# Reciprocal roots on 128x4, spread by turns, and a rotation taken at the eviction, in a two-layer hybrid mixer

## The chip, the cores and the metric

The kernel runs on one core of a Trainium2 chip. The metric is device time in microseconds (us), smaller is better. Three runs of the kernel before gave 2074.2, 2075.43 and 2074.64 us; their median is 2074.64 us. All times in this document are of this one core. PE is TensorE, DVE is VectorE, ACT is ScalarE, POOL is GpSimd.

## What is computed

Two layers of a hybrid mixer on 512 positions of width 1024, then a final norm. The parts that the change touches are the two norms of a layer, the retention branch with its rotation and its per-head normalization, and the retention gate:

```python
def rms_norm(x, g):
    y = x32 * lax.rsqrt(jnp.mean(x32 * x32, axis=-1, keepdims=True) + EPS)
    return (y * g)

def rotary(x, pos, rot_dim, theta):      # halves x1, x2 of each head
    return concat([x1 * cos - x2 * sin, x2 * cos + x1 * sin, rest])

def retention_mixer(z, gn_g):            # 4 heads of 128
    zq, zk, zv, zg = split(z, 4)
    q, k = rotary(zq, ...), rotary(zk, ...) * (dk ** -0.5)
    ...                                  # chunked causal retention -> o
    mu, var = mean(o), mean(square(o - mu))      # per position and head
    o = ((o - mu) * lax.rsqrt(var + EPS)) * gn_g
    return o * jax.nn.silu(zg)

def hybrid_layer(x, ...):
    h = rms_norm(x, norm1_g)
    z = h @ w_in                         # all branches' projections
    y_a, y_b, y_c, y_d = conv, attention, retention, pool branches
    merged = sum over branches of (branch @ w_branch) * sigmoid(z_gate + b_gate)
    x = x + merged @ w_o
    h = rms_norm(x, norm2_g)
    u_gate, u_val = split(h @ w_up, 2)
    return x + (silu(causal_dwconv(u_gate)) * u_val) @ w_down
```

## The kernel before

Features lie on the 128 partitions, the 512 positions on the free axis, so a "tile" is 128 features by 512 positions and fills one PSUM bank. Each projection tile is 8 chunks of three matmuls (`product`, L1189 to L1191): high weights by high data, high weights by low data, low weights by high data. PE walks a fixed list of weight groups: 12 of stage A (`A_TILES`: compressed keys and values, keys, values, four query tiles q0 to q3, the attention gate, an empty "pad"), 32 of stage B (`B_TILES`: the retention tiles rq, rk, rv, rg of each head, the convolution's c, h, b and the pool's u), then the branch merge, the output projection, the up projection (U) and the down projection. ACT makes the high half of each weight group (`ahead`, L456), POOL the low half (L434), DVE evicts each accumulator bank (`take`, L721) multiplied by `rstd`, the norm's reciprocal root, which stands as a full 128x512 tile with one value per column, the same on all partitions.

Norm: PE multiplies a matrix of ones by the 128x512 sums of squares (`sum_squares`, L1257), which gives the column sum on all 128 partitions; ACT takes the square root of 128x512 (`root`, L462), DVE the reciprocal of 128x512 (`inverse_root`, L752). That is done twice per layer (`sumsq1` after tile 2 of stage A, `sumsq2` after the first up tile). The retention heads do the same with L1435 (PE), L590 (ACT) and L968, L971 (DVE, in two halves), four times per layer.

Stage B runs attention (scores, softmax, values) and retention between the quarters of its projection tiles. A table `SIDE` has a slot for each quarter of each of the 32 tiles (slot 4b to 4b+3 for tile b); every engine walks the slots in order and does its own part of each step found there. So the table fixes the order on PE, DVE and ACT, and semaphores count the uses of shared things: two score banks `s` (list `S_USES`, a use may begin when the use two before it is freed), two turn banks `t`, two accumulators `acc` (`acc_free`).

The retention rotation (L757 to L765, `rotate`) takes the evicted rq or rk, has its two halves of 64 partitions exchanged into `rot` by two DMAs that ACT issues (L487, L488), multiplies `rot` by sine, the tile by cosine, and adds: three DVE operations in slots of the tile after next. The attention's own rotations of k0, k1 and q0 to q3 in stage A have the same three operations.

At the end of stage A, DVE evicts tile 10 (the attention gate), rotates q3, finishes the compressed keys (`kc`, L855), makes `center` (L856), reads the pad (L858), and then does step `gate` (L864), which frees the score bank that PE needs for its step `cmp_keys` (L1343).

Of the kernel before, what the change touches and what calls it, by code (L numbers as in the profile page):

```python
# [23 lines left out]
F32 = mybir.dt.float32  # L24
# [5 lines left out]
P = 128  # L30
S = 512
# [76 lines left out]
for _h in range(RH):  # L108
    _n0 = RET_SLOT[_h]
    for _m in range(QT):  # L110
        SIDE[_n0 + _m].append(("ret_scores", _h, _m))
        SIDE[_n0 + _m + 1].append(("ret_values", _h, _m))
    SIDE[_n0 + 5].append(("ret_gate", _h))
    SIDE[_n0 + 6].append(("ret_var", _h))
    SIDE[_n0 + 7].append(("ret_inverse", _h))
    SIDE[POOL_SLOT[_h]].append(("pool", _h))
for _h in range(RH):
    SIDE[RET_SLOT[_h] + (11, 8, 8, 10)[_h]].append(("ret_end", _h))
    SIDE[RET_SLOT[_h] + (12, 9, 9, 12)[_h]].append(("ret_hi", _h))
    SIDE[RET_SLOT[_h] + (14, 10, 10, 14)[_h]].append(("ret_split", _h))  # L120
# [4 lines left out]
for _b in range(B_GROUPS - 1):  # L125
    for _k in range(4):
# [4 lines left out]
        if B_TILES[_b][0] in ("rq", "rk") and _k < 2:  # L131
            SIDE[4 * (_b + 2) + (1 if B_TILES[_b][0] == "rq" else 0) + _k].insert(0, ("rotate", B_TILES[_b], _k))
# [6 lines left out]
S_USES = ["sumsq1", "hid_k", "hid_v", "kc", "vc", "kc_swap"]  # L139
S_USES += [_e for _e in SEQUENCE if _e[0] in ("gate", "cmp_keys", "cmp_scores", "scores", "ret_scores", "ret_var", "pool")]  # L140
S_USES += ["sumsq2"]
# [8 lines left out]
for _slot in SIDE:  # L150
    for _e in _slot:
        if _e[0] in ("cmp_scores", "scores", "ret_gate", "ret_var", "ret_hi", "attn_hi") or _e[0] == "conv" and _e[2] == 2 or _e[0] == "ret_values" and _e[2] == QT - 1:
            A_MADE.append(_e)
# [29 lines left out]
def build(nc, xT, weights, vec, w1, pool_w, consts, decay, out):  # L183
    with ExitStack() as ctx:
# [41 lines left out]
        rg_t = at("rg_t", [P, S], F32, W + 14 * KB)  # L226
# [20 lines left out]
        ssq = at("ssq", [P, S], F32, R + 10 * KB)  # L247
        R2 = R + 12 * KB
# [17 lines left out]
        half_b = small[:, 112:144]  # L266
        pad_out = small[:, 144:146]
# [43 lines left out]
        root_ready = sem("root_ready")  # L311
        ssq_zero = sem("ssq_zero")
# [38 lines left out]
        ROT_DMA = 16 * (3 * 4 + RH * 2)  # L351

        def rot_value(L, name):
            i = ROT[name] // 2
            return L * ROT_DMA + 16 * (4 * (i + 1) if i < 3 else 12 + 2 * (i - 2))
# [89 lines left out]
        def _(act):  # L445
# [12 lines left out]
            def root(use, L):  # L458
# [3 lines left out]
                nc.scalar.activation(rstd[:, :], s_of(use)[:, :], ACT.Sqrt, bias=C("eps", 1),  # L462
                                     scale=1.0 / D).then_inc(root_ready, 1)

            def rotate_partners(L, name):
# [16 lines left out]
                else:  # L482
                    act.wait_ge(acc_free, 1 + L * TILES + (A_GROUPS + B_TILES.index(name) + 2))
                    before = [n for n, k in ROT.items() if k == i - 2][0]
                    act.wait_ge(v_made, v_count(L, before))
                    src = (rq if name[0] == "rq" else rk)[:, name[1] % 2, :]
                    act.dma_start(dst[0:64, :], src[64:128, :]).then_inc(rot_ready[i % 2], 16)  # L487
                    act.dma_start(dst[64:128, :], src[0:64, :]).then_inc(rot_ready[i % 2], 16)  # L488
# [21 lines left out]
            with act.Fori(0, LAYERS) as L:  # L510

                for g in range(A_GROUPS):
# [4 lines left out]
                    if 1 <= g <= 4:  # L517
                        act.wait_ge(acc_free, 1 + L * TILES + g)
                        nc.scalar.activation((k_cmp[:, :], v_cmp[:, :], kT[:, 0, :], kT[:, 1, :])[g - 1], acc[(g - 1) % 2][:, :],
                                             ACT.Copy).then_inc(acc_free, 1)  # L520
                    for name in ("k0", "k1", "q0", "q1", "q2", "q3"):
# [10 lines left out]
                for b in range(B_GROUPS):  # L532
                    ahead(L, A_GROUPS + b)
                    if 0 < b and B_TILES[b - 1][0] in ("rq", "rk"):
                        rotate_partners(L, B_TILES[b - 1])
# [12 lines left out]
                    for n in range(4 * b, 4 * b + 4):  # L548
                        for e in SIDE[n]:
# [28 lines left out]
                            elif e[0] == "ret_gate":  # L578
# [32 lines left out]
                def up(i, g, loop=None):  # L611
                    for k in range(2):
# [7 lines left out]
                        if i is None and k == 0:  # L620
                            root("sumsq2", L)
# [1034 lines left out]
```

## Time and profile before

| | us |
|---|---|
| median of three runs | 2074.64 |
| the profiled execution, own time | 2072.95 |
| its span, first to last instruction | 2071.1 |
| PE busy in the span | 2043.2 (99%) |
| DVE busy | 1209.7 (58%) |
| ACT busy | 685.6 (33%) |
| POOL busy | 917.5 (44%) |

The profiled execution's own time is 1.69 us below the median of the runs. "Busy" of PE counts from the start of a matmul to its modelled end; matmuls overlap, so what one costs is read from the distance between the starts of its neighbours. A row of the timeline gives start and duration in us, engine, line, operation, the names written and read, shapes, a count, and in brackets how long the engine was idle before it and what it waited for.

### The profile page before, as it was taken

To read this page: it belongs to the slowest core of one execution; us is meant where nothing else is said; L and a number is where in the kernel's file an instruction comes from. 1 tells how busy PE (TensorE), PEld (TensorE's weight loads), DVE (VectorE), ACT (ScalarE), POOL (GpSimd) and SP (SyncE) were. 2 spreads that over 40 slices of the span, in tenths; PEclk is the share of its full clock that TensorE was granted. 3 is DMA by queue.
4 is the path that set the end of the run, shared out by engine and by line. 5 is a ranking of instruction groups with operands and counts; after the bars stand their busy time and mean duration, and the time that the engine had idled before them with its cause. 6 is when DMAs were issued, how large, how long until landed. Compare 5 with 4: busy or idle time off the path is not lost.

```text
span 2071.1 us, 31913 instructions
## 1 busy us (share of the span) xinstructions
PE 2043.2 (99%) x9800; PEld 1637.2 (79%) x9800; DVE 1209.7 (58%) x1799; ACT 685.6 (33%) x1007; POOL 917.5 (44%) x672
## 2 busy tenths in 40 slices
PE   9999999999999999999999999999999999999997
PEld 7777677888888888888887777778888888888886
DVE  7766865422327888862267677572322378888522
ACT  4355533323232322222233554333323232222222
POOL 3422233444445555545544212335444455555552
PEclk9999999999999999999999999999999999999998
DMA  5311132222232223223233112322223223232233
GB/s 210 99 60 52 55 91 91 96 92 101 91 101 92 96 97 101 92 94 111 93 126 96 53 51 64 95 89 95 101 91 101 91 93 101 92 101 96 100 105 108
DMA packets 57432, 194.90 MB, mean 94 GB/s; under 512 B 7040, under 2 KB 7552, under 8 KB 57216
## 3 DMA queue, kind: packets, MB, share of 16 engines
q1 hardware_dynamic: 52576, 186.17, 26.8%
q10 hardware_dynamic: 4768, 7.61, 1.5%
q8 instruction: 49, 0.80, 0.2%
q14 instruction: 39, 0.32, 0.1%
HBM read 186.67 MB, written 2.10 MB: 91 GB/s over the span
## 4 chain that ended last, share of the span: by engine, by line
PE 93%; DVE 4%; issue 1%; ACT 1%; DMA 0%; ACTq 0%; SPq 0%; DVEq 0%
PE acc L1189 28%; PE acc L1191 28%; PE acc L1190 28%; PE o L1389 2%; PE s L1363 2%; PE t L1371 1%; PE o L1428 1%; PE s L1418 1%; PE t L1409 0%; DVE win_k L779 0%; DMA w_raw<-weights_dram 0%; PE s L1444 0%; PE s L1435 0%; DVE rstd L752 0%; DVE sc L721 0%
## 5 line engine op out<-in xcount | busy, mean ns | idle before, releaser
L434 POOL TENSOR_TENSOR w_lo<-w_raw,w_hi 128x512 fp32r<-128x512 f32 x668 | 917.3, 1394 | 1129.6 <-ACT w_hi L456 1114.0
L1189 PE MATMUL acc<-xg_hi,w_hi 128*128 128x512 f32 x1904 | 769.5, 404 | 6.5 <-DVE sc L721 3.6
L1191 PE MATMUL acc<-xg_hi,w_lo 128*128 128x512 f32 x1904 | 742.9, 390 | 0.0
L1190 PE MATMUL acc<-xg_lo,w_hi 128*128 128x512 f32 x1904 | 741.8, 390 | 0.0
L456 ACT ACTIVATE w_hi<-w_raw 128x1024 fp32r<-128x1024 f32 x336 | 355.1, 1057 | 777.5 <-PE acc L1191 740.3
L1189 PEld LDWEIGHTS acc<-xg_hi,w_hi 128*128 128x128 f32 x1904 | 357.4, 188 | 116.5 <-issue 33.4
L1190 PEld LDWEIGHTS acc<-xg_lo,w_hi 128*128 128x128 f32 x1904 | 357.8, 188 | 77.1 <-issue 6.7
L1191 PEld LDWEIGHTS acc<-xg_hi,w_lo 128*128 128x128 f32 x1904 | 357.3, 188 | 76.4
L1066 DVE TENSOR_TENSOR work<-acc,rstd 128x512 f32<-128x512 f32 x64 | 44.1, 690 | 256.1 <-PE acc L1191 256.1
L1189 PE MATMUL acc<-act_hi,w_hi 128*128 128x512 f32 x352 | 136.9, 389 | 0.0
L1190 PE MATMUL acc<-act_lo,w_hi 128*128 128x512 f32 x352 | 136.9, 389 | 0.0
L1191 PE MATMUL acc<-act_hi,w_lo 128*128 128x512 f32 x352 | 136.9, 389 | 0.0
L1072 DVE SCALAR_TENSOR_TENSOR work<-work,acc 128x512 f32<-128x512 f32 x64 | 44.0, 687 | 103.1 <-PE acc L1191 103.1
L1160 DVE SCALAR_TENSOR_TENSOR x<-acc,x 128x512 f32 x16 | 11.1, 693 | 158.6 <-PE acc L1191 158.6
L1189 PE MATMUL acc<-y_hi,w_hi 128*128 128x512 f32 x256 | 99.6, 389 | 0.0
L1190 PE MATMUL acc<-y_lo,w_hi 128*128 128x512 f32 x256 | 99.6, 389 | 0.0
L1191 PE MATMUL acc<-y_hi,w_lo 128*128 128x512 f32 x256 | 99.6, 389 | 0.0
L624 ACT ACTIVATE work<-work 128x512 f32<-128x512 f32 x44 | 27.8, 632 | 190.3 <-DVE work L1115 190.3
L924 DVE COPY pT<-t 128x128 f32<-128x128 f32 (+3 forms) x128 | 56.8, 484 | 53.2 <-PE o L1389 53.1
L1191 PEld LDWEIGHTS acc<-act_hi,w_lo 128*128 128x128 f32 x352 | 66.1, 188 | 13.8
L1189 PEld LDWEIGHTS acc<-act_hi,w_hi 128*128 128x128 f32 x352 | 66.1, 188 | 13.7
L1190 PEld LDWEIGHTS acc<-act_lo,w_hi 128*128 128x128 f32 x352 | 66.1, 188 | 13.7
(208 smaller groups left out, 2238.1 us busy)
## 6 DMA issues: line engine op xcount, KB each, us to landing
w_raw<-weights_dram SPq DMA_DIRECT2D x339, 512.0 KB, 3.3
x<-xT_dram SPq DMA_DIRECT2D x8, 256.0 KB, 5.9
rot<-rq ACTq DMA_DIRECT2D x16, 128.0 KB
rot<-rk ACTq DMA_DIRECT2D x16, 128.0 KB
dec<-decay_dram ACTq DMA_DIRECT2D x8, 256.0 KB, 3.3
out_dram<-x SPq DMA_DIRECT2D x8, 256.0 KB, 2.7
con<-consts_dram SPq DMA_DIRECT2D x1, 1406.0 KB, 10.5
w1k<-w_dram SPq DMA_DIRECT2D x2, 512.0 KB, 8.7
```

Of the source, the lines that this page charges most:

```text
L434: nc.gpsimd.tensor_tensor(w_lo[:, slot, part], w_raw[:, slot, part], w_hi[:, slot, part].bitcast(F32), ALU.subtract).then_inc(lo_ready, 1)
L456: nc.scalar.activation(w_hi[:, slot, :], w_raw[:, slot, :], ACT.Copy).then_inc(hi_ready, 1)
L624: nc.scalar.activation(work[:, 2, :], work[:, 1, :], ACT.Tanh, scale=0.5).then_inc(silu_ready, 1)
L924: t_end(ve.tensor_copy(pT[:, u % 2, 0:w], t_of(e)[:, 0:w]), e)
L1066: ve.tensor_tensor(work[:, n, :], acc[n % 2][:, :], rstd[:, :], ALU.mult).then_inc(acc_free, 1)
L1072: ve.scalar_tensor_tensor(out=work[:, n, :], in0=work[:, n, :], scalar=1.0, in1=acc[n % 2][:, :], op0=ALU.add, op1=ALU.mult).then_inc(acc_ ...
L1189: mm(tile, w_h, right_hi, start=first, stop=False)
L1190: mm(tile, w_h, right_lo, start=False, stop=False)
L1191: return mm(tile, w_l, right_hi, start=False, stop=last)
L1363: mm(b[:, 0:w], qT[r, h % 4, qi * P:(qi + 1) * P], kT[r, br, 0:w], start=True, stop=True).then_inc(s_done, 1)
L1371: ins = nc.tensor.transpose(b[:, k * P:(k + 1) * P], pr_of(u)[:, k * P:(k + 1) * P], ident)
L1389: ins = mm(o_bank[qi % 2][d, j * P:(j + 1) * P], v[:, d], p[:, half, :], start=(br == 0 and k == 0), stop=(br == 1 and k == qi + 1))
```

## The change

Four things change.

1. The column sums are computed as four products of one column each: each 128-position block of the squares is the loaded operand, one column of ones the streamed one. Positions then lie on partitions and the sums are 128x4. ACT's root and DVE's reciprocal work on 128x4. Then PE turns each of the four columns, repeated 128 times, by a transpose (`spread_root`, `ret_spread`), which gives the 128x512 tile back. For the norms ACT copies it into `rstd`; for retention DVE reads it from the score bank in `ret_end`.
2. Once per layer, between `kc` and `center`, DVE makes `cos_rms` and `sin_rms`, `rstd` times cosine and sine. rq and rk are evicted times `cos_rms`; ACT copies the two halves from the accumulator bank crosswise into `rot` (two copies of 64x512, in place of two DMAs) and frees the bank; DVE multiplies `rot` by `sin_rms` and adds, both in the last slot of the next tile.
3. ACT's tangent of the retention gate (`ret_tanh`) moves from slot 5 to slot 2 of a head, DVE's use of it (`ret_gate`) from 5 to 4.
4. `ret_end`, `ret_hi` and `ret_split` get other slots.

The diff, cut to its core:

```diff
+    SIDE[_n0 + 2].append(("ret_tanh", _h))
+    SIDE[_n0 + 4].append(("ret_gate", _h))
     SIDE[_n0 + 6].append(("ret_var", _h))
     SIDE[_n0 + 7].append(("ret_inverse", _h))
+    SIDE[_n0 + 8].append(("ret_spread", _h))
...
-    SIDE[RET_SLOT[_h] + (11, 8, 8, 10)[_h]].append(("ret_end", _h))
+    SIDE[RET_SLOT[_h] + (9, 9, 9, 9)[_h]].append(("ret_end", _h))
...
-            SIDE[4 * (_b + 2) + (1 if B_TILES[_b][0] == "rq" else 0) + _k].insert(0, ("rotate", B_TILES[_b], _k))
+    if B_TILES[_b][0] in ("rq", "rk"):
+        SIDE[4 * (_b + 1) + 3].insert(0, ("rotate", B_TILES[_b]))
...
-                nc.scalar.activation(rstd[:, :], s_of(use)[:, :], ACT.Sqrt, bias=C("eps", 1),
+                nc.scalar.activation(root4, s_of(use)[:, 0:QT], ACT.Sqrt, bias=C("eps", 1),
                                      scale=1.0 / D).then_inc(root_ready, 1)
+            def root_spread(use, L):
+                act.wait_ge(s_done, s_use(L, use))
+                nc.scalar.activation(rstd[:, :], s_of(use)[:, :], ACT.Copy).then_inc(rstd_ready, 1)
...
+            def swap_halves(L, tile):
+                T, i = A_GROUPS + B_TILES.index(tile), ROT[tile]
+                act.wait_ge(v_made, v_count(L, ("took", *tile)))
+                nc.scalar.activation(rot[0:64, i % 2, :], acc[T % 2][64:128, :], ACT.Copy)
+                nc.scalar.activation(rot[64:128, i % 2, :], acc[T % 2][0:64, :], ACT.Copy).then_inc(acc_free, 1)
...
+                def inverse_root(n):
+                    dve.wait_ge(root_ready, 2 * L + (n + 1))
+                    s_end(ve.reciprocal(root4, root4), use, wait=True)
+                    alone(dve)
+                    dve.sem_inc(inverse_ready, 1)
+                    dve.wait_ge(rstd_ready, 2 * L + (n + 1))
...
                 def rotate_ret(e):
-                    rotate(e[1], (rq if kind == "rq" else rk)[:, h % 2, :], "cos_r", "sin_r", (e[2],))
+                    dve.wait_ge(acc_free, 1 + L * TILES + (T + 2))
+                    then(ve.tensor_tensor(r, r, sin_rms[:, :], ALU.mult))
+                    v_end(ve.tensor_tensor(z, z, r, ALU.add), e[1])
...
                 v_end(ve.tensor_tensor(kc[:, 0:NCMP], kc[:, 0:NCMP], kc_rot[:, 0:NCMP], ALU.add), "kc")
+                ve.tensor_tensor(cos_rms[:, :], rstd[:, :], C("cos_r", S), ALU.mult).then_inc(chain, 1)
+                then(ve.tensor_tensor(sin_rms[:, :], rstd[:, :], C("sin_r", S), ALU.mult))
                 v_end(ve.scalar_tensor_tensor(out=center[:, :], ...
...
-                    then(ve.reciprocal(pT[:, 1, 0:S // 2], pT[:, 1, 0:S // 2]))
-                    s_end(ve.reciprocal(pT[:, 1, S // 2:S], pT[:, 1, S // 2:S]), ("ret_var", e[1]), wait=True)
+                    s_end(ve.reciprocal(ret_inv, ret_inv), ("ret_var", e[1]))
...
+                    if kind in ("rq", "rk"):
+                        v_end(ve.tensor_tensor((rq if kind == "rq" else rk)[:, i % 2, :], acc[T % 2][:, :], cos_rms[:, :], ALU.mult),
+                              ("took", kind, i), wait=True)
...
-                    mm(b[:, :], ones, ssq[:, :], start=True, stop=True).then_inc(s_done, 1)
+                    for t in range(QT):
+                        ins = mm(b[:, t:t + 1], ssq[:, t * P:(t + 1) * P], ones[:, 0:1], start=True, stop=True)
+
+                def spread_root(use, value):
+                    pe.wait_ge(inverse_ready, value)
+                    b = s_begin(use)
+                    for t in range(QT):
+                        ins = nc.tensor.transpose(b[:, t * P:(t + 1) * P], spread(root4[:, t:t + 1], [[0, P]]), ident)
...
-                                   norm=("sumsq1", L * 16 + DC, 3) if g == 2 else None)
+                                   norm=("sumsq1", L * 16 + DC, 3, sum_squares) if g == 2 else
+                                   ("spread1", L * 2 + 1, 1, spread_root) if g == 3 else None)
...
+                def ret_spread(e):
+                    pe.wait_ge(s_free, 1 + s_use(L, ("ret_var", e[1])) + 1)
+                    b = s_begin(e)
+                    for t in range(QT):
+                        ins = nc.tensor.transpose(b[:, t * P:(t + 1) * P], spread(ret_inv[:, t:t + 1], [[0, P]]), ident)
```

`spread2` is placed in the second up tile in the same way, after its second quarter.

Two places show the order. On PE in tile 3 of stage A, between its second and third quarter, the program before has nothing but the tile's own matmuls:

```order
L1189 MATMUL acc<-xg_hi,w_hi 128x512
L1190 MATMUL acc<-xg_lo,w_hi 128x512
L1191 MATMUL acc<-xg_hi,w_lo 128x512
L1209 REGISTER_ALU
L1189 MATMUL acc<-xg_hi,w_hi 128x512
```

In the changed program the wait for the reciprocal, the wait for a score bank and the four turns stand there:

```order
L1223 MATMUL acc<-xg_hi,w_hi 128x512
L1224 MATMUL acc<-xg_lo,w_hi 128x512
L1225 MATMUL acc<-xg_hi,w_lo 128x512
L1296 ISA
L1274 REGISTER_ALU
L1300 MATMUL s<-con,small 128x128 x4
L1243 REGISTER_ALU
L1223 MATMUL acc<-xg_hi,w_hi 128x512
```

The four turns (L1300) are new on PE's queue, and the 12 matmuls of the tile's second half stand behind them. On DVE at the end of stage A, from the last step of q3's rotation to the attention gate's step, the program before has:

```order
L765 TENSOR_TENSOR qT<-qT,rot 128x512
L855 TENSOR_TENSOR kc<-kc,kc_rot 128x31
L856 SCALAR_TENSOR_TENSOR center<-con 128x128
L857 REGISTER_ALU
L858 COPY small<-acc 128x2
L726 REGISTER_ALU
L864 TENSOR_SCALAR gates<-s 128x96
```

and the changed one:

```order
L789 TENSOR_TENSOR qT<-qT,rot 128x512
L883 TENSOR_TENSOR kc<-kc,kc_rot 128x31
L884 TENSOR_TENSOR cos_rms<-rstd,con 128x512
L886 TENSOR_TENSOR sin_rms<-rstd,con 128x512
L681 REGISTER_ALU
L887 SCALAR_TENSOR_TENSOR center<-con 128x128
L888 REGISTER_ALU
L889 COPY small<-acc 128x2
L745 REGISTER_ALU
L895 TENSOR_SCALAR gates<-s 128x96
```

Two operations of 128x512 stand between `kc` and the step that frees the score bank (`gates`, L864 before, L895 now).

## Rows read from the trace of the kernel before

**Rows 1.** The page's first part: busy us and share of each engine.

```profile
PE 2043.2 (99%) x9800; PEld 1637.2 (79%) x9800; DVE 1209.7 (58%) x1799; ACT 685.6 (33%) x1007; POOL 917.5 (44%) x672
```

**Rows 2.** PE's waits: line, releaser, us in total, times, longest.

```profile
PE t L1371 <- DVE cmp_pT L938: 4.0, 4, 1.6
PE acc L1189 <- DVE sc L721: 3.6, 4, 1.3
PE o L1428 <- DVE pr L949: 2.4, 2, 1.2
...
PE t L1281 <- DVE sc L721: 0.7, 2, 0.3
```

**Rows 3.** PE timeline around the column sum of a retention head (L1435).

```profile
295.22 0.39 PE L1191 MATMUL acc<-xg_hi,w_lo 128*128 128x512 f32 x1
295.45 1.02 PE L1435 MATMUL s<-pT,con 128*128 128x512 f32 x2
...
296.54 0.39 PE L1190 MATMUL acc<-xg_lo,w_hi 128*128 128x512 f32 x1
```

**Rows 4.** PE timeline around four float32 products of 128 columns (L1409).

```profile
279.42 1.05 PE L1409 MATMUL t<-center,rv_T 128*128 128x128 f32 x8
...
280.55 0.40 PE L1190 MATMUL acc<-xg_lo,w_hi 128*128 128x512 f32 x1
```

**Rows 5.** The final norm's products of one column (L1529), one line's view.

```profile
L1529 PE MATMUL s<-con,ssq x8: 334/352/353, 2059.1 to 2060.5; 128*128 128x1 f32 x8
```

**Rows 6.** Busy time by stretch; PEclk stands before the DMA share.

```profile
34.00:56.50 22.50, 20.90 (x141) 17.23 (x140) 21.23 (x22) 4.73 (x5) 12.25 (x8) 1.00 0.27 80
2059.00:2061.00 2.00, 1.83 (x8) 1.74 (x8) 1.15 (x2) 1.58 (x3) 0.00 (x0) 0.53 0.00 0
```

**Rows 7.** Timeline of PE's weight loads: sixteen loads of 31 columns (L1310).

```profile
68.27 0.26 PEld L1310 LDWEIGHTS s<-w2v,small 64*31 64x31 f32 x16
```

**Rows 8.** PE timeline around four turns of 128x128 (L1281).

```profile
62.04 0.60 PE L1281 MATMUL t<-con,sc 128*128 128x128 f32 x4
...
62.71 0.39 PE L1190 MATMUL acc<-xg_lo,w_hi 128*128 128x512 f32 x1
```

**Rows 9.** Timeline of ACT and DVE: the norm's root, first norm and final norm.

```profile
30.17 0.69 ACT L462 ACTIVATE rstd<-s,con 128x512 f32<-128x512 f32 x1
...
30.89 3.35 DVE L752 RECIPROCAL rstd<-rstd 128x512 f32<-128x512 f32 x1 [3.92 <-ACT rstd L462]
...
2060.92 0.26 ACT L644 ACTIVATE rstd<-s,con 128x4 f32<-128x4 f32 x1 [0.40 <-PE s L1529]
2061.22 0.18 DVE L1170 RECIPROCAL rstd<-rstd 128x4 f32<-128x4 f32 x1 [0.93 <-ACT rstd L644]
```

**Rows 10.** PE timeline, stage A, both layers: before and after PE's longest wait.

```profile
54.94 0.30 PE L1272 MATMUL s<-win_v,w1v 128*64 128x62 f32 x1
56.51 0.47 PE L1189 MATMUL acc<-xg_hi,w_hi 128*128 128x512 f32 x1 [1.27 <-DVE sc L721]
...
1079.14 0.47 PE L1189 MATMUL acc<-xg_hi,w_hi 128*128 128x512 f32 x1 [0.85 <-DVE sc L721]
```

**Rows 11.** DVE timeline, end of stage A, first layer.

```profile
80.81 0.69 DVE L761 TENSOR_TENSOR rot<-rot,con 128x512 f32<-128x512 f32 x1
81.42 1.79 DVE L763 TENSOR_TENSOR qT<-qT,con 128x512 f32<-128x512 f32 x1
...
84.83 1.26 DVE L855 TENSOR_TENSOR kc<-kc,kc_rot 128x31 f32<-128x31 f32 x1
86.02 0.28 DVE L856 SCALAR_TENSOR_TENSOR center<-con 128x128 f32<-128x128 f32 x1
...
86.29 0.24 DVE L864 TENSOR_SCALAR gates<-s 128x96 f32<-128x96 f32 x1
```

**Rows 12.** The same stretch on POOL and on PE.

```profile
84.33 3.12 POOL L434 TENSOR_TENSOR w_lo<-w_raw,w_hi 128x512 fp32r<-128x512 f32 x2
...
87.15 1.09 PE L1343 MATMUL s<-qT,kc 64*32 64x512 f32 x16
```

More of the change, by code:

```diff
@@ L136 @@
 SEQUENCE = [_e for _slot in SIDE for _e in _slot]
-S_USES = ["sumsq1", "hid_k", "hid_v", "kc", "vc", "kc_swap"]
-S_USES += [_e for _e in SEQUENCE if _e[0] in ("gate", "cmp_keys", "cmp_scores", "scores", "ret_scores", "ret_var", "pool")]
-S_USES += ["sumsq2"]
+S_USES = ["sumsq1", "spread1", "hid_k", "hid_v", "kc", "vc", "kc_swap"]
+S_USES += [_e for _e in SEQUENCE if _e[0] in ("gate", "cmp_keys", "cmp_scores", "scores", "ret_scores", "ret_var", "ret_spread", "pool")]
+S_USES += ["sumsq2", "spread2"]
 T_USES = ["v_slc", "v_win"]
@@ L159 @@
             V_MADE.append(("u", _e[1]))
-        if _e[0] == "rotate" and _e[2] == 1:
+        if _e[0] == "rotate":
             V_MADE.append(_e[1])
+    if _n % 4 == 3 and B_TILES[_n // 4][0] in ("rq", "rk"):
+        V_MADE.append(("took", *B_TILES[_n // 4]))
 V_MADE += ["branches"]
@@ L247, in build @@
         ssq = at("ssq", [P, S], F32, R + 10 * KB)
+        cos_rms = at("cos_rms", [P, S], F32, R + 10 * KB)
         R2 = R + 12 * KB
@@ L748, in v_end @@
                         dve.wait_ge(v_made, v_count(L, name))
-                def inverse_root(use, n):
+                def inverse_root(n):
+                    use, spread_ = f"sumsq{n + 1}", f"spread{n + 1}"
                     dve.wait_ge(root_ready, 2 * L + (n + 1))
-                    ins = ve.reciprocal(rstd[:, :], rstd[:, :])
-                    s_end(ins, use, wait=True)
+                    s_end(ve.reciprocal(root4, root4), use, wait=True)
+                    alone(dve)
+                    dve.sem_inc(inverse_ready, 1)
+                    dve.wait_ge(rstd_ready, 2 * L + (n + 1))
+                    made["s"] += 1
+                    dve.sem_inc(s_free, 1)
                 def rotate(name, z, cos, sin, parts=(0, 1)):
@@ L1434, in ret_var @@
                     last_wait()
-                    mm(b[:, :], ones, pT[:, 1, :], start=True, stop=True).then_inc(s_done, 1)
+                    for t in range(QT):
+                        ins = mm(b[:, t:t + 1], pT[:, 1, t * P:(t + 1) * P], ones[:, 0:1], start=True, stop=True)
+                    ins.then_inc(s_done, 1)
+                def ret_spread(e):
+                    pe.wait_ge(s_free, 1 + s_use(L, ("ret_var", e[1])) + 1)
+                    b = s_begin(e)
+                    last_wait()
+                    for t in range(QT):
+                        ins = nc.tensor.transpose(b[:, t * P:(t + 1) * P], spread(ret_inv[:, t:t + 1], [[0, P]]), ident)
+                    ins.then_inc(s_done, 1)
                 def pool(e):
@@ L1534, in _ @@
             ins.then_inc(spread_ready, 1)
[L1538 removed]
+CHAIN_LAYER, CHAIN_J, CHAIN_F, CHAIN_D = 161, 4, 15, 2
 def _constants():
```

71 lines of the change are left out of this document (39 added, 32 removed).

## The prediction, made before the changed kernel was run

> **What bounds the kernel now.** I read the page's first part, then PE's waits, then the timelines at the places where the change adds or removes something. PE is busy for 99% of the span [rows 1], and its listed waits for another engine are few: 4.0, 3.6, 2.4 and 0.7 us in both layers together for the four that lie in stages A and B [rows 2]. So every instruction put on PE's queue lengthens the program by its whole price, and work taken from DVE or ACT pays only where PE waits for that work. In the rows the reader is to see (1) what a short float32 product and a turn cost on PE, by the distance of neighbouring starts, and (2) which of PE's few waits the change reaches. A matmul of a projection starts 0.23 us after the one before (295.22 to 295.45, rows 3); I use 0.227, since a chunk of three takes 0.68.
>
> **Column sums on PE, 12 uses (2 norms and 4 heads, 2 layers).** Before, a use is 2 passes of 512 columns: from its start to that of L1190 behind it 296.54 - 295.45 = 1.09, of which one own step of 0.227 is the tile's, so 0.86 us [rows 3]. After, it is four products of one column, which run as 8 passes, each with its own load of 128x128 float32 weights. The nearest rows: four products of 128 columns (8 such loads) cost 280.55 - 279.42 - 0.23 = 0.90 us [rows 4]. Here a pass streams few columns, but it still must load. The operation itself stands in the trace once, in the final norm: 8 passes start from 2059.1 to 2060.5, about 1.45 us for 7 steps, 0.207 each, at a granted clock of 0.53 [rows 5, 6]; at full clock that is about half, 0.104, so 8 take 0.83. I take 0.90, the row measured at full clock in the stream of the tiles, and keep 0.83 as the low end. Sum: 12 x (0.90 - 0.86) = +0.5 us, bounds -0.4 and +0.5. So the narrower form wins nothing on PE.
>
> The Trainium skill bears on this ("TensorE: Matmul & The Clock Gate"): its section "Back-to-back issue gap" gives about 60 cycles, 25 ns, for a matmul of 1 to 64 columns, by which a use would cost 0.2 us and the term be -7.9; its section "LDWEIGHTS" gives columns / 1.2 ns, 107 ns for 128, by which it would cost 0.85 and the term be -0.1. The rows side with the second.
>
> **The spreads, 12 uses, all new on PE.** Four turns cost 62.71 - 62.04 - 0.23 = 0.44 us [rows 8]. 12 x 0.44 = +5.3 us. Nothing on PE hides it. Do they wait for the reciprocal too? In stage A the turns stand 12 matmuls, 2.7 us, behind the sums. ACT's root can't start before 30.17 (its start now), takes 0.26 on 128x4 instead of 0.69, the reciprocal 0.18 instead of 3.35 [rows 9]; ready at about 30.7, PE there at about 31.2. For the heads the turns stand two quarters behind the sums, 2.7 us, and ACT has only the root ahead of them. I put the waits at zero; if that cover is gone, each costs what it is late by, some 0.5 us.
>
> **What the earlier reciprocal gives back.** DVE is saturated from 34 to 56.5 us, 21.2 of 22.5 us [rows 6], and that chain starts at the reciprocal's end, 30.89 + 3.35 = 34.2. After: turns done at about 31.9, ACT's copy to `rstd` some 0.6 (as other ACT copies of this size), so 32.5: 1.7 us earlier. The waits at its end are PE's for the eviction at L721: 0.7 us in two places for the turn of the values (L1281, rows 2), and the long one: PE starts its last compression product at 54.94 and the next tile at 56.51, where 0.11 later was possible: 1.46 us lost, and in layer 2 the same place has 0.42 less idle, so 1.04 [rows 10]. DVE also has the k rotations' DMAs on its way, which start with it. I take all of it, -3.2 us; PE itself arrives 0.4 later there, which helps. The low end of this gain is -2.2, if DVE meets POOL more often. What is late next: the other two of the four L721 waits, 0.76 each, are the gate tile's eviction right behind its own last matmul; they stay.
>
> **The two new products before the gate step.** `cos_rms` and `sin_rms` stand between `kc` and `center`. Queued behind them on DVE are `center`, the pad's copy and `gates`; waiting for `gates` is PE's `cmp_keys`, whose second score bank is the one that step frees. Now DVE ends `kc` at 86.09 and `gates` at 86.53 [rows 11]; PE comes at 87.15 [rows 12]: slack 0.62 us. The two products take at least 2 x 0.69 = 1.38 (the uncontended row of L761), so PE waits at least 0.76. But POOL is at work on the weights until 84.33 + 3.12 = 87.45 [rows 12], and a DVE product of two SBUF tiles that meets it takes 1.79 instead of 0.69, 1.10 more (L763; `kc`, 31 columns, took 1.26 in the same way) [rows 11]. One of the two meets it: 1.86 us. If both do: 2.96. I take 1.86 in each layer, +3.7 us, since POOL's span covers the start of the pair and not its end; bounds +1.5 and +5.9. Everything in front of this place is anchored to PE (the eviction of tile 10 waits for PE), so DVE's earlier start is no cover.
>
> The Trainium skill ("SBUF - State Buffer", section "SBUF: two separate sides") calls this pair of ports an exclusive lock that blocks the other for the whole instruction. By it `center`, which has two SBUF inputs too, should also wait, and the term would be up to +5.9. `center` took 0.28 inside POOL's stretch, so here the row doesn't bear that out fully.
>
> **The rest.** The retention tiles lose one DVE product each (16), the heads their 2 x 1.75 us reciprocals, ACT swaps two DMA issues for two copies. None of it is what PE waits for: the remaining waits, 4.0 at L1371 and 2.4 at L1428 [rows 2], come from attention, convolution and pool steps ahead of them in DVE's order and from the eviction of rq, which costs the same with `cos_rms`. The accumulator bank of rq and rk is freed later by two ACT copies, some 1.2 us; PE needs it a whole tile (5.5 us) later. In slot 7 the rotation now stands ahead of `cmp_scale` and delays it by 1.4 us, where I find about 1 us of cover left. The tangent and the moved end steps hide behind PE. All of this: 0.
>
> **Sum.** +0.5 + 5.3 - 3.2 + 3.7 = +6.3 us. Against the profiled execution's own 2072.95 us that is 2079.3; that execution lies 1.69 below the median of the runs, 2074.64, and the forecast is for a median: 2080.9 us. With the bounds: -0.4 + 5.3 - 3.2 + 1.5 = +3.2 to +0.5 + 5.3 - 2.2 + 5.9 = +9.5, so 2077.8 to 2084.1.
>
> **Rivals.**
> A. The one-column products are nearly free, and the change is not slower. Mechanism: a pass is priced by what it streams, and the loads run ahead. For it: sixteen loads of 31 columns took 0.26 us, 0.016 each [rows 7]; 8 such would be 0.13, the first term 12 x (0.13 - 0.86) = -8.8, the sum -3.0, 2071.6 us. Against it: rows 4 and 5, with full loads. It decides (inside 0.2%) from 0.72 us per use, 0.09 per pass. Chance 0.08.
> B. The two products cost nothing, because PE comes to `cmp_keys` later than I think or DVE earlier. Sum +2.6, 2077.2 us. Against it: 1.38 of work into 0.62 of slack. Chance 0.12.
> C. DVE's relief also removes the waits at L1371 and L1428 (6.4 idle and about 0.17 of restart each, 6 of them) and the gate's cost: +2.6 - 7.4 = -4.8, 2069.8 us. Against it: nothing that is removed stands ahead of them. Chance 0.05.
> D. The 3.2 us of stage A don't come (DVE spends the lead waiting for its DMAs), or ACT's new waits make the spreads late at 12 x 0.25: about +9.5, 2084 us and a little more. Chance 0.09.
>
> **How the numbers follow.** The forecast's case has 0.66; 0.08 of that lies at its lower edge, below +4.1 us. 0.2%, 4.1 us, is about what a measurement of this kernel can tell from no change. Slower: 0.58 + 0.09 (D) = 0.67. Same: 0.08 + 0.12 (B) + 0.08 (A) = 0.28. Faster: 0.05 (C). The range takes the case's bounds, B, and D: 2076 to 2085; A and C are left out, and a little at the top.
>
> **What would show it.** What the one-column sums take from the tile's stream: 0.9 by me, under 0.2 by A. The turns: 0.44 each, without idle before them. In stage A no PE wait at the tile after the compression, where 1.27 and 0.85 stand now. A new PE wait for DVE's `gates` before `cmp_keys`, 1.9 us in each layer, 0 by B, 3.0 if POOL meets both. L1371's and L1428's waits unchanged. A wait of PE for the accumulator of rq or rk, or for the reciprocal, would make my "0" wrong; a DVE lead that shrinks before 55 us would be D.

## The result, and the profile after

Thirteen runs of the changed kernel gave a median of 2078.48 us (2076.95 to 2081.39), thirteen of the kernel before on the same chip 2073.87 us (2072.24 to 2077.26). The ratio is 1.0025, 95% interval 1.0018 to 1.0032: the change is slower by 4.6 us. The forecast was 2080.9 us, range 2076 to 2085, and slower by over 0.2%. The time lies in the range; of the step, 6.3 us were forecast and 4.6 came. The rest of the distance, 0.8 us, is the median of before, 2074.64 in the first three runs.

The profiled execution of the changed kernel took 2077.07 us with a span of 2075.3 us (before 2072.95 and 2071.1). First the engines' line of its page, which answers to [rows 1], then PE's waits (columns as in [rows 2]):

```profile
PE 2044.9 (99%) x9920; PEld 1647.8 (79%) x9920; DVE 1165.1 (56%) x1779; ACT 703.2 (34%) x1043; POOL 917.5 (44%) x672
```

```profile
PE t L1416 <- DVE cmp_pT L969: 4.0, 4, 1.6
PE s L1388 <- DVE gates L895: 3.8, 2, 1.9
PE o L1473 <- DVE pr L980: 2.9, 2, 1.5
...
PE acc L1223 <- DVE sc L740: 1.5, 2, 0.8
```

DVE lost 44.6 us of work, and the kernel is slower. L1416 is L1371 of before, unchanged. The wait for `gates` at L1388 is new. L1473 (L1428 before) went from 2.4 to 2.9. The waits for the eviction to `sc` fell from 3.6 us in four places to 1.5 in two, and the one at the turn of the values (L1281 before) is gone.

All kernels here run the same 7920 matmuls of the projection tiles, so two traces can be laid side by side by the number of the matmul, and the length of each stretch compared. This table does that: us between the starts of the same two matmuls. The times in the first column are those of before.

| stretch (from, in before) | before | after | difference |
|---|---|---|---|
| layer 1: first norm and compression (14.7) | 41.78 | 40.39 | -1.39 |
| to the first step behind the gate (56.5) | 31.66 | 33.67 | +2.01 |
| attention (88.2) | 180.11 | 180.26 | +0.15 |
| heads (268.3) | 101.85 | 102.59 | +0.74 |
| second norm (674.0) | 15.13 | 15.61 | +0.48 |
| up, down, change of layer (689.2) | 358.78 | 358.46 | -0.32 |
| layer 2: first norm and compression (1048.0) | 31.73 | 30.82 | -0.91 |
| gate step and attention (1105.0) | 173.15 | 175.13 | +1.98 |
| heads (1278.2) | 114.68 | 115.47 | +0.79 |
| second norm (1696.8) | 19.67 | 20.22 | +0.55 |

The start differs by 0.15, the stretches left out by 0.06 at most. All together they give the 4.1 us between the two executions (2077.07 and 2072.95 us).

Layer 1's first row also holds the scatter of the start. How late the stream of matmuls gets going differs from profile to profile, and a later start shortens PE's wait for `k_cmp` behind it (1.6 us here, 0.6 in a profile that began 1.8 us later). Counted from the next tile on, which leaves that wait out, the stretch is 34.1 to 34.5 us in the three profiles with a wide first norm and 33.1 in the nine with a narrow one. Layer 2's row has no such scatter.

**Sums and turns on PE.** PE's timeline after, a head's column sum and its turns (columns: start us, us, engine, line, operation, tiles):

```profile
272.64 0.95 PE L1481 MATMUL s<-con,pT 128*128 128x1 f32 x8
273.45 0.49 PE L1223 MATMUL acc<-xg_hi,w_hi 128*128 128x512 f32 x1
273.78 0.40 PE L1224 MATMUL acc<-xg_lo,w_hi 128*128 128x512 f32 x1
...
276.32 0.60 PE L1489 MATMUL s<-con,small 128*128 128x128 f32 x4
276.67 0.48 PE L1223 MATMUL acc<-xg_hi,w_hi 128*128 128x512 f32 x1
276.99 0.39 PE L1224 MATMUL acc<-xg_lo,w_hi 128*128 128x512 f32 x1
```

From the sum's start to the tile's second matmul is 1.14 us, less 0.227 is 0.91; the wide sum took 0.86 [rows 3]. The turns take 0.67 - 0.227 = 0.44 us, with no idle ahead of them.

**The gate.** DVE, POOL and PE where [rows 11, 12] stood:

```profile
84.85 0.68 DVE L884 TENSOR_TENSOR cos_rms<-rstd,con 128x512 f32<-128x512 f32 x1
85.45 1.76 DVE L886 TENSOR_TENSOR sin_rms<-rstd,con 128x512 f32<-128x512 f32 x1
87.25 0.29 DVE L887 SCALAR_TENSOR_TENSOR center<-con 128x128 f32<-128x128 f32 x1
...
87.52 0.25 DVE L895 TENSOR_SCALAR gates<-s 128x96 f32<-128x96 f32 x1
```

```profile
80.05 6.61 POOL L444 TENSOR_TENSOR w_lo<-w_raw,w_hi 128x512 fp32r<-128x512 f32 x4 [2.46 <-ACT w_hi L466]
87.28 2.62 POOL L444 TENSOR_TENSOR w_lo<-w_raw,w_hi 128x512 fp32r<-128x512 f32 x2 [0.62 <-ACT w_hi L466]
```

```profile
87.92 1.09 PE L1388 MATMUL s<-qT,kc 64*32 64x512 f32 x16 [1.88 <-DVE gates L895]
...
1112.67 1.09 PE L1388 MATMUL s<-qT,kc 64*32 64x512 f32 x16 [1.89 <-DVE gates L895]
```

Both products start inside POOL's row (80.05 to 86.66), but only the second is lengthened, to 1.76 us; the first takes 0.68. `center` starts at 87.25, when POOL is idle until 87.28. PE waits 1.88 and 1.89 us.

**Stage A.** PE no longer waits behind the compression, and the eviction it waited for starts at 52.70 us instead of 55.68:

```profile
55.05 0.30 PE L1316 MATMUL s<-win_v,w1v 128*64 128x62 f32 x1
55.27 0.50 PE L1223 MATMUL acc<-xg_hi,w_hi 128*128 128x512 f32 x1
```

**The heads.** Four sums and turns cost 4 x 0.48 = 1.92 us of PE's time in each layer's heads, but the stretch grew by only 0.74 and 0.79. So 1.18 us came back in layer 1 and, since layer 2's stretch also holds its longer wait at L1473 (+0.23), 1.36 in layer 2: 2.5 us, from waits that the forecast had not counted. PE's timeline at the turn of a head's values (L1409 before, L1454 after), before and then after:

```profile
308.36 0.39 PE L1191 MATMUL acc<-xg_hi,w_lo 128*128 128x512 f32 x1
308.74 1.16 PE L1409 MATMUL t<-center,rv_T 128*128 128x128 f32 x8
309.66 0.48 PE L1189 MATMUL acc<-xg_hi,w_hi 128*128 128x512 f32 x1
```

```profile
310.01 0.39 PE L1225 MATMUL acc<-xg_hi,w_lo 128*128 128x512 f32 x1
310.24 1.05 PE L1454 MATMUL t<-center,rv_T 128*128 128x128 f32 x8
311.05 0.48 PE L1223 MATMUL acc<-xg_hi,w_hi 128*128 128x512 f32 x1
311.36 0.40 PE L1224 MATMUL acc<-xg_lo,w_hi 128*128 128x512 f32 x1
```

The step from the tile's last matmul to its next is 1.30 us before and 1.04 after. Before, the turn starts 0.38 us behind the last matmul instead of 0.23, and no bracket with idle time stands behind it: a matmul is drawn 0.39 long while the next one normally starts 0.23 after it, so a wait of up to 0.16 us leaves no gap. The queue of weight loads names it. Its waits in the trace of before:

```profile
PEld t L1409 <- DVE rv_T L721: 1.7, 4, 0.4
```

After, no such row is there. The same kind of step shrinks once more behind the eviction of rg (0.79 to 0.68) and at the first values of head 1 (1.71 to 1.44), and two steps near the end of head 3 (361.54 us in before) lose 0.19 us together.

### The profile page after: what moved, and what is told of

It is laid out like the page before. It is cut to its first block, busy times and chain, and to the rows that moved or that the text cites. A ratio compares the mean times of both kernels' runs of the same rounds, so it can differ in the third digit from the quotient of the medians.

```text
span 2075.3 us, 32213 instructions
## 1 busy us (share of the span) xinstructions
PE 2044.9 (99%) x9920; PEld 1647.8 (79%) x9920; DVE 1165.1 (56%) x1779; ACT 703.2 (34%) x1043; POOL 917.5 (44%) x672
## 4 chain that ended last, share of the span: by engine, by line
PE 94%; DVE 3%; issue 1%; ACT 0%; DMA 0%; SPq 0%; DVEq 0%; ACTq 0%
PE acc L1223 29%; PE acc L1225 28%; PE acc L1224 28%; PE o L1434 2%; PE s L1408 2%; PE t L1416 1%; PE o L1473 1%; PE s L1463 1%; PE s L1316 0%; PE t L1454 0%; DMA w_raw<-weights_dram 0%; PE s L1499 0%; PE s L1481 0%; DVE ssq L1122 0%; DVE x L1207 0%
```

## The experiments

Two questions were open: which part of the change gives what, and what the 2.5 us in the heads were. These kernels ran on three chips, each beside the kernel before, and all ratios are to that one on the same chip. Its medians were 2073.39 us (the first four kernels), 2072.74 (the next four) and 2073.44 (the last two), so a time of one group can't be set against one of another to better than 0.7 us, and for effects of 1 us the table of stretches further down decides.

**The products behind the gate** (after, with this edit):

```diff
-                ve.tensor_tensor(cos_rms[:, :], rstd[:, :], C("cos_r", S), ALU.mult).then_inc(chain, 1)
-                then.n += 1
-                then(ve.tensor_tensor(sin_rms[:, :], rstd[:, :], C("sin_r", S), ALU.mult))
 def gate(e):
     s_end(ve.tensor_scalar(gates[:, :, :], ...), e, wait=True)
+    then(ve.tensor_tensor(cos_rms[:, :], rstd[:, :], C("cos_r", S), ALU.mult))
 def scores(e):
     s_end(ve.tensor_tensor_reduce(pr_of(u), ...), e)
+    if u == 1:
+        then(ve.tensor_tensor(sin_rms[:, :], rstd[:, :], C("sin_r", S), ALU.mult))
```

> The changed kernel with the two products with the rotation tables moved behind what TensorE waits for: rstd times cosine behind the evacuation of the gate's product, rstd times sine behind the second scores. Theory (the products stand ahead of the copy of the gates, and the waits of 1.88 and 1.89 us at L1388 are theirs alone): both waits go, 2078.5 - 3.9 = 2074.6 us. Rival (a later step on VectorE, the copies of the compressed keys or the first scores, is late by as much): 2077 to 2078.5 us, with the wait at the compressed scores or at the first transposes.

2073.93 us, ratio 1.0004 (0.9995 to 1.0013). Both waits are gone, and `cmp_keys` (L1388) starts 0.33 us behind the tile's last matmul:

```profile
85.98 0.40 PE L1225 MATMUL acc<-xg_hi,w_lo 128*128 128x512 f32 x1
86.31 1.09 PE L1388 MATMUL s<-qT,kc 64*32 64x512 f32 x16
```

So the gate step explains nearly the whole slowdown: the stretch falls from 33.67 to 31.71 us, and of what follows only the attention stretch grows, by 0.15 us.

**The rotation alone, and the roots alone.** The first is the changed kernel with all roots wide again, the second the changed kernel with the old rotation.

```diff
 # rotation alone: the wide forms of before in norms and heads
-nc.scalar.activation(ret_inv, s_of(e)[:, 0:QT], ACT.Sqrt, ...)
+nc.scalar.activation(pT[:, 1, :], s_of(e)[:, :], ACT.Sqrt, ...)
-                    s_end(ve.reciprocal(ret_inv, ret_inv), ("ret_var", e[1]))
+                    then(ve.reciprocal(pT[:, 1, 0:S // 2], pT[:, 1, 0:S // 2]))       # slot +6
+                    s_end(ve.reciprocal(pT[:, 1, S // 2:S], ...), ..., wait=True)     # slot +7
 # roots alone: the rotation of before
-                        swap_halves(L, B_TILES[b - 1])
+                        rotate_partners(L, B_TILES[b - 1])
```

> The rotation of the change alone: cosine times root at the eviction, halves crossed by ScalarE, tangent earlier; all roots are wide again (one product of ones, Sqrt and reciprocal on 128x512, no turns). The products ahead of the gate cost 3.9 us in either theory. Theory R (the rotation took away the waits of 2.5 us that hid in the heads' stretch): 2073.9 + 3.9 - 2.5 = 2075.3 us. Theory V (the reciprocals of 128x4 took them away): 2073.9 + 3.9 = 2077.8 us. Half each would be near 2076.5.

> The narrow roots of the change alone, with their turns; the retention projections are evicted and rotated as before (two DMAs that cross the halves, three VectorE operations), no products with the tables. Column sums +0.5, turns +5.3, stage A -3.3, no gate wait: 2073.9 + 2.5 = 2076.4 us by theory R, and 2.5 less, 2073.9 us, by theory V (the narrow reciprocals gave the 2.5 us in the heads).

The roots alone: 2073.64 us, ratio 1.0000 (0.9991 to 1.0009). Its heads take 102.58 and 115.45 us, those of the changed kernel 102.59 and 115.47. So the new rotation, with 16 DVE products fewer and no exchange by DMA, is worth nothing there, and the hidden waits went with the reciprocals, theory V. "No gate wait" held in layer 2 only. In layer 1 PE waited 0.61 us for `gates`, with no product in the way, since `center`, which took 0.28 us in before, took 1.42 beside POOL's subtraction:

```profile
85.69 1.42 DVE L878 SCALAR_TENSOR_TENSOR center<-con 128x128 f32<-128x128 f32 x1
```

```profile
80.89 6.07 POOL L442 TENSOR_TENSOR w_lo<-w_raw,w_hi 128x512 fp32r<-128x512 f32 x4 [2.47 <-ACT w_hi L464]
```

```profile
87.49 1.09 PE L1374 MATMUL s<-qT,kc 64*32 64x512 f32 x16 [0.61 <-DVE gates L886]
```

The slack of 0.62 us [rows 11, 12] is thus used up by one such delay. That the heads' waits went with the reciprocals is also seen at the same place (turn of the values, 309.70 to 310.73, 1.03):

```profile
309.70 0.39 PE L1211 MATMUL acc<-xg_hi,w_lo 128*128 128x512 f32 x1
309.93 1.05 PE L1440 MATMUL t<-center,rv_T 128*128 128x128 f32 x8
310.73 0.48 PE L1209 MATMUL acc<-xg_hi,w_hi 128*128 128x512 f32 x1
```

The rotation alone: 2096.82 us, ratio 1.0118 (1.0102 to 1.0133), 21.5 us more than theory R gave and 19.0 more than theory V. Both theories missed: they had it that the parts simply add. The next kernel shows the same, and why.

**Wide heads in the changed kernel** (norms narrow, rotation new; the edit is the first one above, for the heads only).

> The changed kernel with the four heads' roots per layer wide again (one product of ones, reciprocal of 128x512 in two halves, no turns); the two norms of a layer stay narrow and the rotation is the new one. Eight sums and turns less: 8 x 0.48 = 3.9 us. Theory R: 2078.5 - 3.9 = 2074.6 us. Theory V: the hidden waits come back, 2074.6 + 2.5 = 2077.1 us.

2092.99 us, ratio 1.0100 (1.0084 to 1.0115), 15.9 us more than theory V gave. PE's waits begin with one that only this kernel and the rotation alone have:

```profile
PE acc L1225 <- ACT rot L502: 10.3, 4, 3.1
```

Two of the four waits are of 3.1 us and two of 2.0, one of each in a layer. DVE, ACT and PE at one of the longer ones:

```profile
331.58 1.75 DVE L1002 RECIPROCAL pT<-pT 128x256 f32<-128x256 f32 x1 [1.42 <-ACT pT L607]
333.46 1.76 DVE L795 TENSOR_TENSOR rot<-rot,sin_rms 128x512 f32<-128x512 f32 x1
335.25 1.66 DVE L796 TENSOR_TENSOR rq<-rq,rot 128x512 f32<-128x512 f32 x1
336.84 1.74 DVE L997 RECIPROCAL pT<-pT 128x256 f32<-128x256 f32 x1
338.70 0.69 DVE L1082 TENSOR_TENSOR rk<-acc,cos_rms 128x512 f32<-128x512 f32 x1
```

```profile
339.42 0.59 ACT L501 ACTIVATE rot<-acc 64x512 f32<-64x512 f32 x1 [6.12 <-DVE rk L1082]
...
340.03 0.59 ACT L502 ACTIVATE rot<-acc 64x512 f32<-64x512 f32 x1
```

```profile
340.76 0.47 PE L1225 MATMUL acc<-xg_hi,w_hi 128*128 128x512 f32 x1 [3.10 <-ACT rot L502]
```

From 331.58 to 338.58 DVE has two reciprocals and the rotation of rq, 6.9 us of work, ahead of the eviction of rk, and the bank is free only when ACT has copied both halves, at 340.6. PE has the other bank for one tile, about 5.5 us, and comes back at 337.5. In the changed kernel the reciprocal there takes 0.17 us.

Behind the wait TensorE also loses clock: from 342.2 us on eight matmuls start 0.43 us apart instead of 0.23, 1.6 us more, with a granted clock of 0.50, which is the lower level of 1.2 GHz (busy time by stretch, PEclk before the DMA share):

```profile
343.00:344.00 1.00, 1.00 (x4) 0.71 (x3) 0.83 (x2) 0.00 (x0) 1.00 (x1) 0.50 0.00 0
```

The same happens once in layer 2 of this kernel, at 1372.8 us, and three times in the rotation alone; not every one of the waits is followed by it.

**The same, with the rotation's arithmetic behind the next eviction:**

```diff
-        SIDE[4 * (_b + 1) + 3].insert(0, ("rotate", B_TILES[_b]))
+        SIDE[4 * (_b + 2)].insert(0, ("rotate", B_TILES[_b]))
```

> The kernel with wide heads' roots and the new rotation, with VectorE's two rotation products and sums of rq and rk moved behind the next eviction, where they stood ahead of it. Theory (the waits of 10.3 us for the halves that ScalarE copies are VectorE's queue ahead of the eviction of rk: two reciprocals and the rotation of rq, 6.9 us): these waits go, 2093.0 - 10.3 = 2082.7 us or a little less. Rival (the bank is held too long by the eviction and two copies of 0.59 us behind the wide reciprocal in any case): 2088 to 2093 us.

2076.36 us, ratio 1.0017 (1.0008 to 1.0026): 16.6 us less than with the rotation ahead, where the theory had 10.3 or a little more. The steps at the four waits shrink by 11.2 us, the two stretches at the lower clock give 3.2, and a step at the turn of head 0's values, where PE had waited 0.9 us for rv_T in either layer, gives 2.3. The heads fall from 109.68 to 101.27 and from 122.63 to 114.23 us. DVE at the same place:

```profile
330.94 1.75 DVE L997 RECIPROCAL pT<-pT 128x256 f32<-128x256 f32 x1
332.81 0.69 DVE L1082 TENSOR_TENSOR rk<-acc,cos_rms 128x512 f32<-128x512 f32 x1
333.63 0.69 DVE L795 TENSOR_TENSOR rot<-rot,sin_rms 128x512 f32<-128x512 f32 x1
```

With wide reciprocals the rotation's two operations, which also met POOL (1.76 and 1.66 us for 0.69 each), decided over the whole tile. So the rotation at its new place needs the narrow reciprocals; the two are not separate gains or losses.

The attention stretch of layer 1 is 1.6 us longer (181.83 us) than in the changed kernel. That is not the place of the rotation: PE waits for nothing there, but from 89 to 93 us it runs at the lower clock, behind its wait of 1.89 us for `gates`:

```profile
90.00:91.00 1.00, 1.00 (x3) 0.72 (x3) 1.00 (x3) 0.00 (x0) 0.18 (x1) 0.50 0.00 0
```

In the changed kernel the granted clock stayed at 1.00 behind the same wait, and so it did in layer 2 of this one.

**Only the first norm narrow** (the kernel before, with the changed root, reciprocal and turn for `sumsq1` alone):

> The kernel before with one part of the change alone: the first norm of each layer has its root and reciprocal on 128x4, with the turn in the next group. If stage A's gain is that of the earlier reciprocal and needs nothing else of the change, the stretch from the first norm to the gate is 1.4 us shorter in layer 1 and 0.9 us in layer 2, net of sums and turns: 2073.4 - 2.3 = 2071.1 us. If it came together with another part (a changed phase of the weight split), it is smaller or absent: 2073.4 us or above.

2071.52 us, ratio 0.9994 (0.9985 to 1.0003). Stage A gives what it gave in the changed kernel, 40.43 and 30.82 us. The whole is 1.2 to 1.4 us instead of 2.3, since other stretches grew by a little (attention 180.37, heads 102.03 and 115.01 us).

**Only DVE's order changed** (the kernel before, wide roots, no turns):

```diff
-    SIDE[RET_SLOT[_h] + (11, 8, 8, 10)[_h]].append(("ret_end", _h))
-    SIDE[RET_SLOT[_h] + (12, 9, 9, 12)[_h]].append(("ret_hi", _h))
-    SIDE[RET_SLOT[_h] + (14, 10, 10, 14)[_h]].append(("ret_split", _h))
+    SIDE[RET_SLOT[_h] + (12, 8, 8, 10)[_h]].append(("ret_end", _h))
+    SIDE[RET_SLOT[_h] + (13, 9, 9, 12)[_h]].append(("ret_hi", _h))
+    SIDE[RET_SLOT[_h] + (14, 16, 16, 14)[_h]].append(("ret_split", _h))
```

In this kernel and the next one head 0 is closed with head 1's gate, since the tile `rg` has been taken again by then; the operations are the same, so the time can be read.

> The kernel before with nothing but VectorE's order changed in the heads' stretch: the low half of heads 1 and 2 is formed behind the evictions of the next head's rv and rg instead of ahead of them (it took 1.8 us there), and the end of head 0 behind the next head's first scores. Wide roots, no turns. Theory Q (the waits that hid in the heads' stretch are VectorE's queue ahead of an eviction, whatever fills it): eight or so waits of 0.27 and 0.10 us go, about -2.0 us, 2071.4 us, and the steps of TensorE at the next head's turn of the values fall from 1.30 to 1.03 us. Rival (they belong to the reciprocals as such, their use of VectorE and the buffers): no change, 2073.4 us, steps of 1.30 us as before.

2071.23 us, ratio 0.9993 (0.9984 to 1.0002). The median is 1.5 us below before, which the interval alone doesn't tell from no change; the stretches of the heads are 100.90 and 113.55 us, 0.95 and 1.13 less than before, -2.1 as theory Q had it. DVE before, where the low half (L983) met POOL and held the eviction of rv, and then in this kernel:

```profile
306.07 1.80 DVE L983 TENSOR_TENSOR y_lo<-pT,y_hi 128x512 fp32r<-128x512 f32 x1
308.00 0.69 DVE L721 TENSOR_TENSOR rv_T<-acc,rstd 128x512 f32<-128x512 f32 x1
```

```profile
306.48 0.68 DVE L721 TENSOR_TENSOR rv_T<-acc,rstd 128x512 f32<-128x512 f32 x1
```

The next turn's step on PE is 308.77 to 309.80, 1.03 us. The wide reciprocals still stand there, 1.74 and 1.75 us. So these waits are DVE's queue ahead of an eviction, whatever fills it, and reordering removes 2.1 of the 2.5 us without a turn. What it leaves are the two steps at 361.54 us in each layer (0.4 us together), which shrink only where the heads' reciprocals are narrow.

**Both together, and then with head 0's own gate.** First the two parts together:

> Both: the kernel before with a narrow first norm and the changed order of VectorE in the heads. If the two gains are independent: 2073.4 - 2.3 - 2.0 = 2069.1 us, faster than both kernels; otherwise between 2071 and 2073.4.

2069.57 us, ratio 0.9982 (0.9973 to 0.9991). Then the form in which head 0 ends where it did, so that its own gate is used:

```diff
 # first norm narrow, and
-    SIDE[RET_SLOT[_h] + (14, 10, 10, 14)[_h]].append(("ret_split", _h))
+    SIDE[RET_SLOT[_h] + (14, 16, 16, 14)[_h]].append(("ret_split", _h))
```

> The kernel before with a narrow first norm, and with the low halves of heads 1 and 2 formed behind the evictions of the next head's rv and rg; head 0 ends where it did before. Of the gains of the two parts (2.3 and 2.1 us in the stretches), only head 0's waits (0.27 us per layer) stay: 2069.6 + 0.5 = 2070.1 us, faster than both kernels. If moving the low half alone does not free the evictions, nothing is gained in the heads: 2071.5 us.

2070.13 us, ratio 0.9983 (0.9974 to 0.9992): faster than both kernels, by 3.3 us than the one before. The time is as expected, but not by the parts: the heads gave 0.92 us instead of 1.6, since head 0's waits did not only stay but grew (the step at head 1's first values went from 1.71 to 1.90 us).

**Is the new rotation worth anything with all else in its way removed?** First norm narrow, second norm and heads wide, products behind the gate, rotation behind the next eviction, the low halves behind:

> What is left of the change when every part that cost time is taken out or moved: narrow first norm, new rotation with the products behind the gate and the rotation's arithmetic behind the next eviction, wide second norm and heads, low halves of heads 1 and 2 behind. If the new rotation is worth something once nothing stands in its way, it is below 2070 us; if it is neutral, it stands with the kernel above, about 2070 us, plus what the rotation of head 0 costs the first attention units where it now stands (1.6 us in the run with the later rotation): 2071.5 us.

2070.52 us, ratio 0.9987 (0.9978 to 0.9996). The same as the kernel above within the measurement: the stretches of the heads are 101.33 and 114.22 against 101.37 and 114.24 us. The 1.6 us in layer 1's attention did not come back (180.39), though the rotation stands where it did: without the wait for `gates`, the clock did not fall. The new rotation is neutral.

The stretches of the kernels, in us, from the starts of the same matmuls as in the first table:

| | norm 1 | to gate | attention | heads 1 | norm 2 | norm 1, L2 | gate, att. L2 | heads 2 |
|---|---|---|---|---|---|---|---|---|
| before | 41.78 | 31.66 | 180.11 | 101.85 | 15.13 | 31.73 | 173.15 | 114.68 |
| after | 40.39 | 33.67 | 180.26 | 102.59 | 15.61 | 30.82 | 175.13 | 115.47 |
| products behind the gate | 40.42 | 31.71 | 180.41 | 102.58 | 15.64 | 30.82 | 173.30 | 115.47 |
| roots alone | 39.63 | 32.40 | 180.38 | 102.58 | 15.64 | 30.82 | 173.24 | 115.45 |
| rotation alone | 40.31 | 33.65 | 180.35 | 111.33 | 15.14 | 31.74 | 175.22 | 122.56 |
| heads wide | 40.43 | 33.68 | 180.39 | 109.68 | 15.63 | 30.82 | 175.20 | 122.63 |
| heads wide, rotation later | 40.43 | 33.67 | 181.83 | 101.27 | 15.63 | 30.82 | 175.12 | 114.23 |
| first norm narrow | 40.43 | 31.73 | 180.37 | 102.03 | 15.16 | 30.82 | 173.27 | 115.01 |
| DVE order alone | 41.53 | 31.70 | 180.07 | 100.90 | 15.15 | 31.74 | 173.17 | 113.55 |
| first norm narrow, DVE order | 40.41 | 31.71 | 180.34 | 100.93 | 15.13 | 30.82 | 173.30 | 113.89 |
| first norm narrow, low halves behind | 40.43 | 31.73 | 180.37 | 101.37 | 15.15 | 30.82 | 173.27 | 114.24 |
| all else out of the rotation's way | 40.40 | 31.71 | 180.39 | 101.33 | 15.14 | 30.82 | 173.30 | 114.22 |

Three entries of layer 1 need a word: in the rotation alone (norm 1, 40.31 with a wide norm) and the roots alone (39.63) the stream began 1.8 us later than in before, and the 32.40 of the roots alone holds the wait of 0.61 us for `gates`.

## Why the prediction was right, and where it was off

- **Column sums, +0.5.** 0.91 us against the 0.90 taken, 0.86 before. Right. Rival A (nearly free, 0.13) is out, and so is C: L1371's wait stayed and L1428's grew. In the final norm the same eight passes took 1.83 us before, at a granted clock of 0.53, the lower level of 1.2 GHz [rows 6]. In the changed kernel's profile they ran at 2.4 GHz and took 1.05 (busy time by stretch, PEclk before the DMA share):

```profile
2063.00:2064.40 1.40, 1.05 (x8) 0.97 (x8) 1.27 (x3) 1.38 (x2) 0.00 (x0) 1.00 0.00 0
```

- **Turns, +5.3.** 0.44 each and no wait for the reciprocal, in norms and heads. Right, also where it was said what covers them.
- **Stage A, -3.2.** The stretches give -1.39 and -0.91; each holds a sum and a turn, +0.48, so the gain is 1.87 + 1.39 = 3.3 us. Right, and the kernel with only the first norm narrow has the same two stretches. Layer 1's part is good to some 0.4 us, for the reason given below the first table. Rival D is out.
- **Gate step, +3.7.** +2.01 and +1.98 in the stretches that hold it, waits of 1.88 and 1.89 us where 1.86 was taken. Exactly one product met POOL in either layer, though it was the second of the pair and not, as forecast, the first. With both moved behind the gate the kernel takes 2073.93 us. Right; rival B is out.

  The forecast doubted that `center` can be held by POOL, from one row in which it took 0.28 us. That reading was too quick. In all but one of 24 uses in the twelve profiles it took 0.28 or 0.29 us, and in one, the roots alone, 1.42. In before it starts within 0.01 us of one of POOL's subtractions, and in the changed kernel while POOL is idle, so neither row speaks against a lock. The Trainium skill ("SBUF - State Buffer", section "SBUF: two separate sides") has it that whichever of the two operations starts first gets the ports for its whole length; the 1.42 us agree with it.
- **"All of this: 0".** This is the term that was mis-sized. It held that the heads' reciprocals (16 pieces of 1.75 us) are nothing PE waits for, because PE's list of waits had no row for them. The evictions behind them in DVE's queue were late, and PE lost 2.5 us by it. The forecast's sum of 6.3, less 2.5, with 0.45 us more at L1473, 0.3 more at the gate, 0.1 less in stage A, -0.3 at the change of layer and 0.15 at the start, is 4.3; the two executions differ by 4.1. The step that failed is the reading, not the cost: PE's waits at the evictions of rv and rg had to be read from the weight loads' queue, or from the distance of starts (1.30 us where 1.04 would do).
- **Rotation, within the same 0.** It was right that 16 DVE products and the exchange of halves are worth nothing, and that the bank, freed later by two copies, is not waited for; "PE needs it a whole tile (5.5 us) later" was the margin. The kernels with wide heads show how thin it is: with 6.9 us ahead of the eviction the margin is overrun by 3.1 us, and at the other place of each layer by 2.0.
- **L1416 and L1473 unchanged.** L1416 was, 4.0 us. L1473 was not: 1.22 became 1.44 and the like in layer 2, with +0.15 us over the attention stretch. The eviction of rq starts later, for on DVE a copy of 8 columns (L1026 before, L1055 after) takes 1.27 us instead of 0.16. POOL's subtraction started 0.03 us after it before and 0.03 us ahead of it after. DVE and POOL before, then DVE and POOL after:

```profile
254.11 0.16 DVE L1026 COPY sc<-sc 128x8 f32<-128x8 f32 x1
...
254.14 2.96 POOL L434 TENSOR_TENSOR w_lo<-w_raw,w_hi 128x512 fp32r<-128x512 f32 x2 [5.81 <-ACT w_hi L456]
```

```profile
254.83 1.27 DVE L1055 COPY sc<-sc 128x8 f32<-128x8 f32 x1
...
254.80 2.52 POOL L444 TENSOR_TENSOR w_lo<-w_raw,w_hi 128x512 fp32r<-128x512 f32 x2 [5.81 <-ACT w_hi L466]
```

All twelve profiles agree with it: in the ten in which this copy took 1.27 us, in both layers, PE's step at L1473 is 5.02 to 5.04 us, and in the two in which it took 0.16 (before, and DVE's order alone) 4.79 or 4.80. A kernel in which nothing but this copy moved was not run. The order of starts is not the whole of it either: a copy of one column (L1026 at 350.04 us in before) took 0.15 us in the middle of POOL's work.
- **Change of layer, not in the forecast.** One step of 0.74 us became 0.30. It takes 0.30 to 0.74 us over the twelve profiles, and 0.68 in the kernel with the products behind the gate, whose code there is that of the changed kernel. So this looks like scatter between executions, not like the change.

## What to carry to other kernels

On an engine that is busy for 99%, an operation that another engine hands to it must be paid in waits that it removes there, so look for them place by place: here the narrow form gave 3.3 us for 1.0 in the first norm, 2.5 for 3.8 in the heads and nothing for 1.0 in the second norm. Before a new operation is put into another engine's queue, ask who waits for the step behind it, since two products that nobody needed yet cost nearly 4 us there and nothing one step later. And a step that delays an eviction can be moved behind it; reordering alone gave 2.1 us in the heads where the narrow reciprocals gave 2.5, without anything on PE.

## What the hardware showed that was not expected

- Waits of PE under some 0.16 us are not drawn as idle time; the distance of starts shows them (0.38 for 0.23), and the weight loads' queue names them. In the heads such steps, taken over this kernel, were 2.5 us too long.
- A DVE copy of 8 columns took 1.27 us when POOL's operation started 0.03 us ahead of it, 0.16 us when it started 0.03 us behind. `center`, 128x128, took 1.42 us once and 0.28 or 0.29 in its other 23 uses. What an operation costs beside POOL can't be read from one row.
- Behind waits of 1.9 to 3.1 us TensorE's granted clock fell to 0.50 for four to eight matmuls in some places (0.43 us from start to start instead of 0.23) and stayed at 1.00 in others with the same wait. Eight such matmuls cost 1.6 us.
- Eight float32 passes of one column take 0.91 us in the stream, 0.11 each, and eight of 128 columns 0.89 (from 310.24 to the tile's second matmul at 311.36, less 0.23): here the number of columns does not set the time.
